# The delta scan's state as whole 128x128 tiles: banks with zeroed off-diagonal quarters

## The reference, cut to what matters

```python
    def step(s, xs):
        u_n, w_n, k_n, gl_n = xs
        v_new = u_n - w_n @ s
        s_next = s * jnp.exp(gl_n)[..., None, None] + jnp.einsum("bhcd,bhce->bhde", k_n, v_new)
        return s_next, (s, v_new)

    s_final, (s_prev, v_new) = lax.scan(step, s0, (u, w, k_dec, g_last))
    o = jnp.einsum("nbhcd,nbhde->nbhce", qc * jnp.exp(G)[..., None], s_prev) + qk @ v_new
```

## Time and profile before

| | |
|---|---|
| Median of 3 runs | 2463.73 us (2458.98 to 2467.26) |
| Profiled execution, its own time | 2459.26 us |
| Its span, first to last instruction | 2457.4 us |
| Mean granted TensorE clock | 0.961 |
| TensorE / VectorE / ScalarE / GpSimd busy | 93% / 60% / 46% / 5% |
| Scan of layer 0, first L1069 to first L1099 | 412.1 to 443.4 us |
| Scan of layer 1, the same | 1422.1 to 1451.1 us |

### The profile page before, as it was taken

The page is one execution under the profiler, slowest core; times in us unless marked ns, Lnnn a source line. Parts: engine busy times, 40 slices in busy tenths (PEclk is TensorE's granted clock), DMA queues, the critical chain, the costliest instruction groups (busy, mean ns, idle before and its releaser), DMA issues.

```text
span 2457.4 us, 39471 instructions
## 1 busy us (share of the span) xinstructions
PE 2280.8 (93%) x16570; PEld 1877.8 (76%) x16570; DVE 1464.7 (60%) x2152; ACT 1120.6 (46%) x1545; POOL 121.3 (5%) x94
## 2 busy tenths in 40 slices
PE   6998989999998999895978999959999999999997
PEld 4777778777787888784766989948888888888885
DVE  2134667533333222234456675439999999899997
ACT  3224431322233222224244033238778787787785
POOL 0000450000000000000004300000000000000000
PEclk8999999999998999998989999969999999999999
DMA  8882002322204232220300055229899898998994
GB/s 334 331 331 96 1 3 89 120 86 97 73 20 156 88 103 86 86 88 34 103 1 1 4 201 178 86 99 366 341 350 360 334 374 340 348 361 339 350 361 177
DMA packets 63331, 448.40 MB, mean 182 GB/s; under 512 B 7216, under 2 KB 8240, under 8 KB 9520
## 3 DMA queue, kind: packets, MB, share of 16 engines
q1 hardware_dynamic: 60880, 434.86, 46.7%
q10 hardware_dynamic: 2272, 10.97, 1.2%
HBM read 443.71 MB, written 2.10 MB: 181 GB/s over the span
## 4 chain that ended last, share of the span: by engine, by line
PE 85%; DVE 6%; ACT 3%; issue 2%; DMA 2%; PEld 1%; POOL 1%; SPq 0%; ACTq 0%; PEldq 0%; DVEq 0%; POOLq 0%
PE bank L1099 11%; PE bank L1191 10%; PE bank L615 9%; PE bank L596 7%; PE bank L598 7%; PE bank L597 7%; PE bank L1202 5%; PE bank L976 5%; PE bank L701 3%; PE bank L1127 3%; PE bank L1110 3%; PE bank L469 3%; PE bank L756 3%; PE bank L713 2%; PE bank L548 1%
## 5 line engine op out<-in xcount | busy, mean ns | idle before, releaser
L1930 DVE TENSOR_TENSOR wsp_l<-ring,wsp_h 128x1024 fp32r<-128x1024 f32 x528 | 639.4, 1222 | 38.3 <-ACT wsp_h L1284 7.3
L1284 ACT CAST wsp_h<-ring 128x1024 fp32r<-128x1024 f32 x528 | 555.1, 1054 | 142.7 <-PE bank L598 86.5
L596 PE MATMUL bank<-wsp_h,xTs_h 128*128 128x512 f32 x704 | 283.5, 403 | 3.7 <-DVE wsp_l L1930 3.7
L598 PE MATMUL bank<-wsp_h,xTs_l 128*128 128x512 f32 x704 | 276.0, 392 | 0.0
L597 PE MATMUL bank<-wsp_l,xTs_h 128*128 128x512 f32 x704 | 274.6, 390 | 0.0
L2444 DVE TENSOR_TENSOR dsp_l<-ring,dsp_h 128x1024 fp32r<-128x1024 f32 x66 | 80.8, 1225 | 245.8 <-ACT dsp_h L1665 245.8
L1665 ACT CAST dsp_h<-ring 128x1024 fp32r<-128x1024 f32 x66 | 69.0, 1047 | 261.9 <-PE bank L1191 178.5
L1099 PE MATMUL bank<-u_hi,gsp_h 128*128 128x512 f32 (+1 forms) x512 | 180.2, 352 | 0.0
L2355 DVE TENSOR_TENSOR gsp_l<-ring,gsp_h 128x1024 fp32r<-128x1024 f32 x60 | 73.5, 1225 | 166.9 <-ACT gsp_h L1590 166.4
L1099 PE MATMUL bank<-u_hi,gsp_l 128*128 128x512 f32 (+1 forms) x512 | 172.0, 336 | 0.0
L1099 PE MATMUL bank<-x_lo,gsp_h 128*128 128x512 f32 (+1 forms) x512 | 171.7, 335 | 0.0
(11 more groups left out here) (335 smaller groups left out, 4446.0 us busy)
## 6 DMA issues: line engine op xcount, KB each, us to landing
ring<-in_moe_tiles_dram SPq DMA_DIRECT2D x264, 1024.0 KB, 4.8
ring<-in_ada_tiles_dram SPq DMA_DIRECT2D x48, 1024.0 KB, 11.0
ring<-in_ffn_tiles_dram SPq DMA_DIRECT2D x33, 1024.0 KB, 4.8
ring<-in_gate_tiles_dram SPq DMA_DIRECT2D x32, 1024.0 KB, 5.7
ring<-in_in_tiles_dram SPq DMA_DIRECT2D x22, 1024.0 KB, 4.9
arena<-in_branch_tiles_dram ACTq DMA_DIRECT2D x8, 1024.0 KB, 7.5
ring<-in_out_tiles_dram SPq DMA_DIRECT2D x8, 1024.0 KB, 4.8
halfc<-in_halfc_dram SPq DMA_DIRECT2D x1, 1040.0 KB, 17.8
```

Source lines behind the costliest of these rows:

```text
L596: pe.matmul(o, xTs[0][:, kk, :], whi[:, k, :], start=(kk == 0), stop=False)
L598: mm = pe.matmul(o, xTs[1][:, kk, :], whi[:, k, :], start=False, stop=(kk == KD - 1))
L1284: act.copy(wsp[0][:, g % 4, :], half_slot(MOE0, g)).then_inc(s.gq_o.up, 1)
L1930: v.tensor_tensor(wsp[1][:, g % 4, :], half_slot(MOE0, g), wsp[0][:, g % 4, :], ALU.subtract).then_inc(s.gq_pt.up, 1)
```

## The change

The outer products go to the diagonal quarters of a 128x128 tile in `bank[2 + dr]` (at `P * a + CH * hp`), and VectorE fills that tile's other two quarters with zeros before the scan, once for each layer. The state's update then takes the whole tile, one operation for each pair of heads, and in the first step one copy of 128x256 for each direction. The list of instructions behind the scan is as before.

```diff
-                                    mm = pe.matmul(bank[2 + dr][rows[hp], CH * a:CH * (a + 1)], kdec[dr][rows[c], t, CH * hh:CH * (hh + 1)],
+                                    mm = pe.matmul(bank[2 + dr][rows[hp], P * a + CH * hp:P * a + CH * (hp + 1)], kdec[dr][rows[c], t, CH * hh:CH * (hh + 1)],
                                                    vnew[rows[c], 2 * dr + hp, 2 * t + a, :], start=True, stop=True)
...
                 for g in range(4):
                     v.wait_ge(*s.u_mm(g + 1))
-                    v.tensor_copy(vnew[:, g].rearrange("p x n -> p (x n)"), bank[g][:, :]).then_inc(s.u_ok.up, 1)
+                    ins = v.tensor_copy(vnew[:, g].rearrange("p x n -> p (x n)"), bank[g][:, :])
+                    if g >= 2:
+                        link(ins)
+                        for hp in range(2):
+                            at = CH * (1 - hp)
+                            ins = v.memset(bank[g][rows[hp], 0:BW].rearrange("p (a n) -> p a n", a=2)[:, :, at:at + CH], 0.0)
+                        link(ins)
+                        v.sem_inc(s.u_ok.up, 1)
+                    else:
+                        ins.then_inc(s.u_ok.up, 1)
...
                             v.wait_ge(*s.st_s(2 * i + dr + 1))
-                            for a in range(2):
-                                for hp in range(2):
-                                    part = slice(CH * hp, CH * (hp + 1))
-                                    x, upd = S[part, dr, a, part], bank[2 + dr][part, CH * a:CH * (a + 1)]
-                                    if i == 0:
-                                        ins = v.tensor_copy(x, upd)
-                                    else:
-                                        at = 2 * dr + a
-                                        ins = v.scalar_tensor_tensor(x, x, decay_to[part, k % 2, k // 2, at:at + 1], upd,
-                                                                     ALU.mult, ALU.add)
+                            if i == 0:
+                                ins = v.tensor_copy(S[:, dr].rearrange("p a n -> p (a n)"), bank[2 + dr][:, 0:BW])
+                            else:
+                                for a in range(2):
+                                    at = 2 * dr + a
+                                    ins = v.scalar_tensor_tensor(S[:, dr, a, :], S[:, dr, a, :],
+                                                                 decay_to[:, k % 2, k // 2, at:at + 1],
+                                                                 bank[2 + dr][:, P * a:P * (a + 1)], ALU.mult, ALU.add)
                             ins.then_inc(s.st_S.up, 1)
```

## The result

The changed kernel took 2441.52 us (median of 4 runs, 2439.48 to 2447.79), the kernel before 2465.49 us: ratio 0.991, 95% interval 0.9882 to 0.9939, so 22 us less by that ratio (15 to 29; the medians themselves differ by 24). It was compared a second time, beside 11 runs of the kernel before: 2447.57 against 2462.41 us, ratio 0.9942 (0.9925 to 0.9959), 14 us less (10 to 18). The first comparison is the less certain one: its 4 runs of the kernel before have a median 3 to 4 us above the other three groups of 29, 11 and 11 runs (2461.55, 2462.41 and 2461.66 us). All runs on record together, 13 of the changed kernel and 56 of the one before, have medians of 2446.9 and 2462.2 us, 15 us apart. The direction of the forecast was right, its size and its range (2447 to 2461) were not.

What follows compares the result with a forecast made beforehand. VectorE's state updates, taking turns with TensorE in the two scans, were taken as the bound. Gains of 4.5 + 4.2 = 8.7 plus 0.3 for a shorter slow stretch made 9.0 us: median 2463.73 becomes 2454.7, range 2447 to 2461.

Steps and rivals of the forecast that it cites:

- layer 0, first step: Scan's first step in layer 0, updates as copies: TensorE, at half clock, keeps most of the saving; gain 0.3 us.
- layer 0, three full steps: Layer 0 steps at full clock with outputs: TensorE becomes late next, ending the step at 3.3 us; gain 0.6 us each.
- layer 0, three steps with additions: Layer 0 steps with output additions (L2341), all VectorE's chain before, under 3.3 us afterwards: gain 0.85, 0.7 and 0.85 us.
- layer 1, first step: Layer 1's first scan step: ScalarE's last copy of w is late next; second direction's products come 0.6 us earlier.
- layer 1, two half-clock steps: Layer 1's third and fourth scan steps, clock granted 0.50: TensorE paces the state products; gains 0.8 and 0.5 us.
- layer 1, the fifth: Layer 1's next step begins about 3 us earlier and falls into the slow stretch: minus 0.3 instead of plus 0.6.
- zeros: Memsets before each layer's scan, 0.45 us per bank: hidden by existing waiting, cost nothing; without cover 0.9 us a layer.
- TensorE's floor: Full-clock scan step with outputs: TensorE's own work, 1.28 + 2.04 = 3.3 us, limits the gain to 0.6 us a step.
- Rival A: Layer 1's scan keeps 2.4 GHz: 6.9 us gained in that layer, 11.4 in all, 2452.3 us; chance 0.20.
- Rival B: TensorE or instruction supply keeps more, or zeros lose cover: 6 or 4 us remain, about 2458.7; chance 0.22.
- C: Slower: half clock through both scans after a longer stop before the scan, 2473 us; chance 0.05.
- One reading behind the scan: Gates' products (L1099): third piece needed 11 us later, VectorE has it after 4.5 us, so the gain passes on undiminished.

Runs made afterwards that it cites:

- e3: The kernel before plus four filler 128x128 matmuls in each scan step, ahead of TensorE's wait for the first direction's state: 2460.63 us, ratio 0.9993.

## Why the prediction was wrong in size

Step by step, for the gain in the scans (us):

| term | predicted | measured (first profile of each kernel) |
|---|---|---|
| layer 0, first step | 0.3 | 1.91 |
| layer 0, three full steps | 0.6 each | 1.04 to 1.07 |
| layer 0, three steps with additions | 0.85, 0.7, 0.85 | 1.08, 1.09, 1.31 |
| layer 1, first step | 0.6 | 0.48 |
| layer 1, second step | 1.1 | 1.24 |
| layer 1, two half-clock steps | 0.8, 0.5 | 1.88, 2.36 |
| layer 1, the fifth | -0.3 | 1.05 |
| layer 1, the last two | 0.6, 0.85 | 1.05, 1.33 |
| zeros | 0 | 0 |
| sum | 8.7 | 18.0 |

The mechanism was right: the update's chain goes, TensorE is late next, the zeros are hidden, ScalarE's copy of w binds layer 1's first step (ACT L1570 in the chain above), and what is gained passes on behind the scan. Two terms were mis-sized: the floor that TensorE's own work puts under a step, and the half clock, which was taken as fixed. Of the 9.3 us between the two sums, 3.8 lie in the nine full or added-to steps (six in layer 0, three in layer 1) and 5.5 in the four steps that the forecast held at half clock (the fifth of layer 1 has a part in each).

*TensorE's floor.* "1.28 + 2.04 = 3.3 us": I took 1.02 us from L1051's start to what follows for each direction, and added it twice. That counts four groups of matmuls (L1051 and L1058 of each direction), about 0.5 us each, one behind another. In the trace before each direction waited for its own state, so they could not stand otherwise. When both states are ready the middle two, the first direction's L1058 and the second's L1051, run at the same time, and the four take 1.51 us. Measured: 2.88 us a step, 2.69 after reordering. The trace before had shown the same thing for the small products, where the second direction's L1069 and the first's L1077 take turns:

```profile
434.91 0.22 PE L1069 MATMUL bank<-arena 64*64 64x64 f32 x1
434.91 0.22 PE L1077 MATMUL bank<-arena 64*64 64x64 f32 x1
434.92 0.27 PE L1069 MATMUL bank<-arena 64*64 64x64 f32 x2
```

*The clock.* I held layer 1's half-clock stretch fixed in place and even let a fifth step fall into it, and gave its going a chance of 0.20. It was gone in three of the changed kernel's five profiles. Its layer 1 took 19.65 us without it, 23.09 us with 10.2 us of it and 24.67 us with 13.7 us; the kernel before took 29.02 and 29.63 us with the same two lengths. So with an equal stretch on both sides the gain in layer 1 is 5.9 or 5.0 us, against the forecast's 4.2, and 9.4 to 10 us where the stretch is on the side of before alone. With full clock on both sides it would be about 7.6 us, an estimate from e3's 27.2, which has work added. In layer 0 before's first profile had 3.4 us of half clock, from 415.17 on, its second none: its first step was 4.59 and 3.45 us. So 1.14 of that step's 1.91 us are the clock. The other 0.77 are more than the 0.3 of the forecast, which called TensorE "at half clock" at 414.8, before the clock had fallen. With the same clock on both sides the scans gain 7.4 us and 5.0 to 5.9 us, 12 to 13 in all and not 8.7: the floor was too high even there. The rest of the 18.0 is half clock that the kernel before met in its first profile and the changed kernel did not.

Rival A named the second of these, at 11.4 us in all. Its own steps add up to 7.35 us in layer 1, not 6.9, so 11.9; what is missing beyond that is the floor and layer 0's half clock. Rival B pointed the wrong way, C did not come up. One reading behind the scan was for layer 0 alone: in layer 1 the gates' products are half as wide, 0.12 us each, so the third piece is needed after 5.5 us and not 11. VectorE had it 3.4 us after the start, so nothing came of it.

How far does it reach to the total? The scans' means over five profiles of the changed kernel are 22.71 and 21.34 us, over two of before 30.86 and 29.33: 16.1 us less, between the two comparisons of 22 and 14 us and inside both intervals. Why the first comparison is higher is not shown. One of its four runs of the changed kernel was profiled; that profile had the full clock and, by the table, 1.4 us less outside the scans. But the fifth profile also had the full clock in both scans, and took 2446.91 us where the third took 2435.23: 12 us of scatter lie in stages that the change does not touch. The scan began between 412 and 422 us over all profiles, whatever the kernel.

## What to carry to other kernels

When a chain leaves an engine, the next engine's floor is not the sum of start-to-next intervals read while it was waiting; count its instructions at the spacing they have where it is saturated (here 32 small and 16 larger matmuls, 2.7 to 2.9 us), and look in the trace for groups that already run side by side. On VectorE, short updates split by partition halves paid twice here, by number (0.47 us a step) and by losing the overlap with the neighbour (0.74 us); widening them paid even at the price of computing zeros. Where a stretch shows half clock, price the change with and without it, as two cases of similar weight, and take more than one profile of each kernel before explaining a difference of a few us.

## What the runs showed of the hardware that was not expected

- Two groups of matmuls whose outputs lie in different halves of the partitions (64 columns of weights each) ran side by side: the first direction's L1058 and the second's L1051 both start at 427.24. Those of one direction, in the same half, followed one another. That the halves decide it was not tested.
- Eight 64-column updates took 1.62 us where all started at partition 0 (128 partitions each), and 2.36 us where they alternated between partitions 0 and 64 (64 partitions each).
- TensorE stood still for 0.71 to 1.80 us within the first group of outer products of layer 0's scan in all 18 profiles, while the DMA share of that stretch was anything between 0.00 and 0.93. In six of them it stood still once more in the same scan, for 0.17 to 0.97 us, with a DMA share of 0.90 to 1.03. What it waits for stays open in both.
- The granted clock fell in one profile and not in another of the same kernel, with the same instructions ahead of it.
